# Output weight chunks moved into freed weight columns, 128-wide first scores, two weight waits, value products one place further behind

## The reference

```python
h = rmsnorm(x, norm_g)
proj = einsum('bsd,dp->bsp', h, w_in)          # q, k, v, gate of three groups, 8 heads of 64 each
o_sb = stick_breaking_attention(q, k, v)       # weights from sigmoids and a reverse cumulative product
o_ch = chunked_relpos_attention(norm(q), norm(k), v, rel_bias)   # softmax over own chunk + 8 before
o_fx = forgetting_attention(norm(q), norm(k), v, log_f)          # softmax with a decay, causal
mixed = concatenate([o_sb*silu(g_sb), o_ch*silu(g_ch), o_fx*silu(g_fx)])     # 1536 columns
return x + einsum('bsm,md->bsd', mixed, w_out)
```

## Time and profile before

| what | value |
|---|---|
| time, median of 3 runs | 1063.33 us (1063.33 to 1063.95) |
| time of the profiled execution | 1061.9 us |
| its span in the profile | 1060.1 us |
| granted TensorE clock, mean | 0.998 of full |
| PE busy | 1019.6 us, 96% |
| DVE busy / ACT busy | 680.4 us, 64% / 632.8 us, 60% |
| DMA traffic | 105.50 MB, 100 GB/s on average |

### The profile page before, as it was taken

One profiled execution on the slowest core, in us unless ns is written; L12 is line 12 of the kernel. 1 busy time (PEld: TensorE's weight loads), 2 busy tenths in 40 slices (PEclk: granted clock), 3 DMA queues, 4 the chain that ended last, 5 costly groups with the idle time before them and its releaser, 6 DMA issues.

```text
span 1060.1 us, 16214 instructions
## 1 busy us (share of the span) xinstructions
PE 1019.6 (96%) x5816; PEld 911.5 (86%) x5816; DVE 680.4 (64%) x1272; ACT 632.8 (60%) x1232; POOL 95.9 (9%) x74
## 2 busy tenths in 40 slices
PE   6999999999999999999999999999999997799998
PEld 5989989899899998998998998988988985677887
DVE  4656675765856656657557549789789677667210
ACT  5658775766767767758667667567566555444000
POOL 1210201101111011011011000011011010000000
PEclk9999999999999999999999999999999999999999
DMA  8244152331432413315314204214124137732941
GB/s 247 81 118 135 29 143 54 100 100 46 127 85 63 131 47 100 100 51 134 88 28 125 75 20 125 56 35 126 40 51 132 25 90 197 228 92 80 301 136 40
DMA packets 112944, 105.50 MB, mean 100 GB/s; under 512 B 10048, under 2 KB 83784, under 8 KB 112864
## 3 DMA queue, kind: packets, MB, share of 16 engines
q1 hardware_dynamic: 110432, 104.42, 35.5%
q10 hardware_dynamic: 2432, 0.05, 0.1%
HBM read 62.44 MB, written 19.98 MB: 78 GB/s over the span
## 4 chain that ended last, share of the span: by engine, by line
PE 77%; DVE 11%; ACT 5%; DMA 4%; issue 3%; SPq 1%; ACTq 0%; DVEq 0%
PE psP L1202 37%; PE psO L1294 8%; PE psT L1276 7%; PE psS L1254 4%; PE psP L1206 4%; PE psS L1255 4%; PE psP L1312 3%; PE psP L1342 2%; PE psS L1342 2%; DVE big L987 2%; PE psT L1224 2%; DMA stack<-stack 2%; PE psO L1342 2%; DVE pt L1117 1%; DVE rb L1106 1%
## 5 line engine op out<-in xcount | busy, mean ns | idle before, releaser
L1202 PE MATMUL psP<-big 128*128 128x384 f32 (+1 forms) x2304 | 478.8, 346 | 0.7 <-issue 0.5
L1202 PEld LDWEIGHTS psP<-big 128*128 128x128 f32 x2304 | 395.8, 189 | 7.2 <-issue 0.9
L1117 DVE TENSOR_TENSOR pt<-psT,pt 128x512 fp32r<-128x512 f32 (+1 forms) x224 | 143.3, 642 | 144.7 <-ACT pt L929 144.0
L929 ACT ACTIVATE pt<-psT 128x512 fp32r<-128x512 f32 (+1 forms) x224 | 124.9, 558 | 124.1 <-PE psT L1276 123.1
L1206 PE MATMUL psP<-big 128*128 128x512 f32 x576 | 157.2, 405 | 0.0
L1294 PE MATMUL psO<-pt,vst 128*128 128x512 f32 (+3 forms) x576 | 140.1, 343 | 8.4 <-DVE pt L1117 7.6
L1276 PE MATMUL psT<-identr,z 128*128 128x128 f32 x816 | 125.4, 272 | 0.0
L1206 PEld LDWEIGHTS psP<-big 128*128 128x128 f32 x576 | 102.0, 189 | 17.6
L1294 PEld LDWEIGHTS psO<-pt,vst 128*128 128x128 f32 x576 | 99.2, 189 | 20.6 <-issue 10.5
L1090 DVE CUSTOM_DVE_ANT_0 z<-psS,rb 128x640 f32<-128x640 f32 (+7 forms) x128 | 89.3, 698 | 39.5 <-PE psS L1255 20.4
L1276 PEld LDWEIGHTS psT<-identr,z 128*128 128x128 f32 x816 | 101.5, 140 | 15.3
(11 more groups left out here) (113 smaller groups left out, 1090.9 us busy)
## 6 DMA issues: line engine op xcount, KB each, us to landing
stack<-stack SPq DMA_DIRECT2D x192, 128.0 KB, 2.3
wraw<-in_w_in_dram SPq DMA_DIRECT2D x90, 192.0 KB, 2.6
wraw<-in_w_in_dram SPq DMA_DIRECT2D x24, 256.0 KB, 3.6
mixed_scratch<-mst SPq DMA_DIRECT2D x24, 256.0 KB, 2.7
mixed_scratch<-gate SPq DMA_DIRECT2D x24, 256.0 KB, 2.8
wraw<-in_w_out_dram SPq DMA_DIRECT2D x24, 256.0 KB, 2.8
rb<-decay_scratch SPq DMA_DIRECT2D x8, 512.0 KB, 4.1
big<-mixed_scratch SPq DMA_DIRECT2D x8, 512.0 KB, 6.1
```

The source lines that it names most:

```text
L929: nc.scalar.activation(pt[:, ci % PTR, 0, 0:w], psT[:, m % NT, 0:w], ACT.Copy).then_inc(s_hi, 1)
L1117: nc.vector.tensor_tensor(pt[:, ci % PTR, 1, 0:w], psT[:, m % NT, 0:w], pt[:, ci % PTR, 0, 0:w].bitcast(F32), ALU.subtract).then_inc(s_eva ...
L1202: ins = nc.tensor.matmul(dst[:, 0:TOKW - first], hT[a][:, k, i * P:(i + 1) * P], wpair[b][:, k, first:TOKW], start=(k == 0 and q == 0), st ...
```

## The change

Five things change.

1. `score_parts`: the first scores of a head are computed 128 wide instead of 256. The planner's cost of these steps falls with it.
2. `turned_steps`: the products of bank b stand behind the transposes of bank b+2, where it was b+1.
3. The weight waits at a pair's first token tile (except in the first pair): instead of one before each of 8 steps, one before step 0 for chunk 3 and one before step 4 for chunk 7.
4. The output weights: chunks 0 to 5 now go to the q, k, v columns of the input weights, which are free when the last token tile is projected (`s_tk`), and only from chunk 6 on does ACT wait for the gate (`s_gk`). These places and the next four (gate columns) are not one run of 512 columns but two of 256 or four of 128; the matmul reads its moving operand in these pieces (`shaped`). The planned places `WOUT` change: chunks 0 to 5 stand at 0.6 to 3.6, and 6 to 15 from 4.2 on 0.35 apart, where all 16 stood from 4.2 on 0.3 apart.
5. The output products: they may start at 4.2 instead of 5.5, and the two tiles of a pair of tiles no longer alternate step by step; the second starts 2.5 steps behind the first. `MIXF` changes slightly.

```diff
-        return at, [(at, k0 * P, max(w, 256))]
+        return at, [(at, k0 * P, w)]
...
+STAGGER = 2.5
+
+SOON = 6
...
-WOUT = [round(4.2 + 0.3 * c, 2) for c in range(EARLY)]
-FIRST_AT = 5.5
-MIXF = [2.8, 2.8, 7.0, 7.4]
+WOUT = [round(0.6 + 0.6 * c, 2) for c in range(SOON)] + [round(4.2 + 0.35 * c, 2) for c in range(EARLY - SOON)]
+FIRST_AT = 4.2
+MIXF = [2.7, 2.9, 7.0, 7.4]
...
-        seq += [("turn", u, b), ("values", u, b - 1)]
-    return seq + [("values", u, len(banks(u)) - 1)]
+        seq.append(("turn", u, b))
+        if b > 1:
+            seq.append(("values", u, b - 2))
+    return seq + [("values", u, b) for b in range(len(banks(u)) - 2, len(banks(u)))]
...
-    for i, k in [(i + b, k) for i in range(0, len(FIRST), 2) for k in range(MF) for b in range(2)]:
+    order = [(MF * (i // 2) + k + STAGGER * (i % 2) + 0.7 * (i // 2), i, k) for i in range(len(FIRST)) for k in range(MF)]
+    for _, i, k in sorted(order):
...
+        qkv_place = [wpair[i][:, k:k + 2, FW:FW + 256] for i in range(2) for k in range(0, KT, 2)]
+        qkv_place += [wpair[i][:, k:k + 4, FW + 256:TOKW] for i in range(2) for k in range(0, KT, 4)]
+        late_place = [wpair[i][:, k:k + 4, TOKW:WP] for i in range(2) for k in range(0, KT, 4)] + [
+            hT[i][:, k, HALF:SEQ] for i in range(2) for k in range(KT)]
+        places = qkv_place + late_place
...
+                wo[b][k][half] = places[2 * c + b] if c < EARLY else hT[b][:, c - EARLY, 0:HALF]
+
+        def shaped(flat, place):
+
+            return flat if len(place.shape) == 2 else flat.rearrange("p (a b) -> p a b", a=place.shape[1])
...
                     if step[1] == 0:
+                        act.wait_ge(s_tk, KT * PAIRS)
+                    if step[1] == SOON:
                         act.wait_ge(s_gk, KT * PAIRS)
...
-                        if gi == 0:
-                            pe.wait_ge(s_wlo, CHUNK["weights", j, k] + 1)
+                        if gi == 0 and (j == 0 or k % 4 == 0):
+                            pe.wait_ge(s_wlo, CHUNK["weights", j, k if j == 0 else k + 3] + 1)
...
-                            ins = nc.tensor.matmul(psP[:, i % 2, :], mixF[t][a][:, k, :], wo[b][k][c],
+                            ins = nc.tensor.matmul(shaped(psP[:, i % 2, :], wo[b][k][c]), mixF[t][a][:, k, :], wo[b][k][c],
```

More of the change, by code:

```diff
@@ L391, in build @@
         wpair = [big[:, w0 + i * KT * WP:w0 + (i + 1) * KT * WP].rearrange("p (k c) -> p k c", k=KT) for i in range(2)]
-        wo = [[[None] * 2 for _ in range(PAIRS)] for _ in range(2)]
[L395 to L403, removed]
+        qkv_place = [wpair[i][:, k:k + 2, FW:FW + 256] for i in range(2) for k in range(0, KT, 2)]
[3 more added lines that the diff above has]
+        places = qkv_place + late_place
+        wo = [[[None] * 2 for _ in range(PAIRS)] for _ in range(2)]
+        for c in range(24):
+            k, half = wout_at(c)
+            for b in range(2):
+                wo[b][k][half] = places[2 * c + b] if c < EARLY else hT[b][:, c - EARLY, 0:HALF]
+        def shaped(flat, place):
+            return flat if len(place.shape) == 2 else flat.rearrange("p (a b) -> p a b", a=place.shape[1])
         mixF = [[hT[h][:, :, t * P:(t + 1) * P] for h in range(2)] for t in range(FIRST_T)]
@@ L813, in _ @@
                     act.wait_ge(s_wld[CSLOT[c]], 16 * CUSE[c])
-                    nc.scalar.activation(wo[0][pos][half], wplace[CSLOT[c]],
+                    nc.scalar.activation(wo[0][pos][half], shaped(wplace[CSLOT[c]], wo[0][pos][half]),
                                          ACT.Copy).then_inc(s_whi, 1)
@@ L1009, in _ @@
                     dve.wait_ge(s_whi, c + 1)
-                    nc.vector.tensor_tensor(wo[1][pos][half], wplace[CSLOT[c]], wo[0][pos][half].bitcast(F32),
+                    nc.vector.tensor_tensor(wo[1][pos][half], shaped(wplace[CSLOT[c]], wo[1][pos][half]),
+                                            wo[0][pos][half].bitcast(F32),
                                             ALU.subtract).then_inc(s_wlo, 1)
@@ L1341, in _ @@
                         for q, (a, b) in enumerate(((0, 0), (0, 1), (1, 0))):
-                            ins = nc.tensor.matmul(endbank[g % 5], src[:, a, :], wo[b][k][c],
+                            ins = nc.tensor.matmul(shaped(endbank[g % 5], wo[b][k][c]), src[:, a, :], wo[b][k][c],
                                                    start=(k == k00 and q == 0), stop=(k == PAIRS - 1 and q == 2))
```

## The result

The changed kernel takes 1075.11 us (median of 6, 1072.16 to 1079.03) where the kernel before takes 1063.57 on the same chip: ratio 1.0109, 95% interval 1.0088 to 1.0129. It is slower by 11.5 us (1.1%); I had forecast 1048. The profiled execution took 1072.18 us.

What follows compares the result with a forecast made beforehand. PE, busy 96% of the span, and the moments in which it stands were taken as the bound. 1061.9 - 1.7 - 6 - 0 - 7.1 = 1047.1 us; with 1.4 for the median 1048.5, stated as 1048, range 1040 to 1059.

Steps and rivals of the forecast that it cites:

- The value products: Products one bank further behind: half of 11.5 us of PE waits close, 6 us gained; ends 11.5 gain, 3.5 loss.
- rival two: Attention part: blocked ACT starts copies late, DVE idles then lags; the 6 us stay out, 1054.5 us; chance 0.13.
- The output stretch: Early chunks and earlier output products: 16 us lost before, less 8.9 us of other limits, 7.1 us won.
- Chunk waits: Output products: PE's waits for chunk subtractions fall from 10.8 us to under 4.
- the mixed values: Output start: PE waits for their loads, 2.0 us for the first tile, up to 1.0 for the second; sum 3.
- so 2 us: Output, fifth tile: PE waits 2 us for the residual's addition, rows landing 4 to 5 us after issue.
- The clock: Output: granted clock stays 1.00 between 880 and 925 us; the 1.6 us lost at 0.50 before count as won.
- First scores: 24 first scores 128 wide: 0.07 us less a head, 1.7 us gained on PE; ends nothing and 2.8.
- Weight waits: Two waits in place of eight at a pair's first tile: zero, with an end of +1.4 us.
- Rival four (pieces): Output products of chunks 4 to 7: PE reads four pieces like four matmuls; 1057 or 1070 us; chance 0.06.

Runs made afterwards that it cites:

- e1: The changed kernel with the value products back at one bank behind, all other edits kept: 1060.27 us, ratio 0.9966 to the kernel before.
- e2: The kernel before with only the value products two banks behind (units 0 to 43; last four units as before): 1082.34 us, ratio 1.0168.
- e5: The changed kernel with value products one bank behind in units 3, 7, 11 and so on, two behind in the other 36: 1063.41 us, ratio 0.9990.
- e9: The changed kernel with value products two banks behind only in units 3, 7, 11 and so on, one behind elsewhere: 1071.00 us, ratio 1.0093.
- e10: e1 with the next pair's head transposes placed later, behind one more score and one more bank: 1076.28 us, ratio 1.0120 to the kernel before.
- e12: The changed kernel once more, unaltered, for a second profile: profiled execution 1076.94 us.
- e4: The kernel before with the output edits alone (chunk places and times, earlier start, second tile 2.5 steps behind): 1060.63 us, ratio 0.9970.
- e8: e1 with the second residual load issued ahead of mixed values 2 and 3: 1055.52 us, ratio 0.9917 to the kernel before.
- e6: The kernel before with the first scores 128 wide in place of 256, alone: 1063.84 us, ratio 1.0003.
- e7: The kernel before with first scores 128 wide and two weight waits in place of eight: 1063.30 us, ratio 0.9996.

## Why the prediction was wrong, point by point

**The value products: -6 forecast, +15 to +18 measured (e1, e2).** The step that failed reads: "But that dependence stood before as well, and then those transposes came after these products; the copy starts no later than before relative to the products it waits for." Relative to its products it starts no later; relative to everything else on PE it does, because the products themselves moved back behind whatever stood between the banks. In one unit of four that is the head transposes and a score. The sentence ahead of it named what queues behind the blocked copy, "sigmoids, raw copies", and left out the one with the least slack, the head copy: two pairs of transfers and the next pair's scores hang on it. What I had priced at nothing measured 10.3 us of stack waits and 3.9 us of head transposes waiting for a bank. e5 and e9 place all but 2.6 us of the loss in those units, e10 shows that the delay of this chain is enough by itself. By the Trainium skill ("TensorE: Matmul & The Clock Gate", section "Architectural detail", on engine queue depths) ScalarE and VectorE are strictly first in, first out. The trace agrees, with the head copy 2.6 us behind its transposes' start. The gain side was right in kind (7.6 to 1.9 us), and rival two had the blocked ACT, but followed it to DVE and not to the head copy, and priced it as eating 6 us, no more.

**The rest of that loss, the clock.** I had counted the slow clock only where it stood before. Behind small regular waits stand new stretches at 1.2 GHz, outside the output work: five in e2's profile, two in each of e9's, e10's and e12's, none in the changed kernel's first. No step of the sum had a term for it.

**The output stretch: -7.1 forecast, -3.2 measured (e4).** Chunk waits went to nothing and the mixed values cost 2.3 to 3.3 for my 3: right. Mis-sized was "so 2 us" for the residual rows: 5.3 us in e4. I let the rows land 4 to 5 us after issue, and 13 us after SP began the second loads of mixed values. In e4 SP begins those at 900.8, needs 3.5 us to issue the three rows, and DVE adds at 916.96: 9.2 us after the first row's issue and 16 after that of the mixed values. The 3 us between 13 and 16 are about what my wait was short by (3.3):

```profile
907.74 3.51 SPq L674 DMA_DIRECT2D raw<-in_x_dram  x3
...
916.96 0.69 DVE L1161 TENSOR_TENSOR raw<-psP,raw 128x512 f32<-128x512 f32 x1 [4.79 <-DMA raw<-in_x_dram]
```

The clock, which I had forecast at 1.00, missed by as much: I had counted the slow 3.4 us of before as won (1.6 us), and e4's profile has 10.2 us at 0.50 about the two waits, with PE at work in 7.6 of them, which is 3.8 us lost.

```profile
881.20:884.60 3.40, 3.26 (x9) 2.05 (x8) 0.66 (x1) 0.10 (x1) 0.00 (x0) 0.50 1.10 331
915.30:922.10 6.80, 4.30 (x12) 3.55 (x13) 2.40 (x4) 0.60 (x1) 0.00 (x0) 0.50 0.57 143
```

e8 moves the mixed values from ahead of the residual rows to behind them and gets 5.2 us.

**First scores: -1.7 forecast, 0 measured (e6).** The matmuls are as cheap as I said: starts 0.06 and 0.11 us apart in place of 0.115 twice, about 60 ns a head and 1.4 us over 24. Two exposed weight loads, as I had worked them out from the Trainium skill ("TensorE: Matmul & The Clock Gate", section on LDWEIGHTS), would have made 0.21; it is 0.17. What the step left out is that PE then meets its next wait sooner: work taken off an engine need not be time. That this is where the 1.4 us went is argued, not shown.

```profile
303.24 0.22 PE L1269 MATMUL psS<-stack 128*128 128x128 f32 x1
303.30 0.28 PE L1270 MATMUL psS<-stack 128*128 128x128 f32 x1
303.41 2.31 PE L1217 MATMUL psP<-big 128*128 128x384 f32 x12
```

**Weight waits: 0, with an end of +1.4. Right (e7).** **Rival four (pieces) is false:** successive output products that read four pieces start 233 ns apart at full clock (median of 40), those that read one piece 231 (77), and 231 before. The slower case came by another way than the one I gave 0.06.

**The sum.** By the parts, -6 became +15 (e1), -7.1 became -3.2 (e4) and -1.7 became 0 (e6), some 27 us in all. That is the distance from 1048 to 1075, so no large term is missing.

## What to carry to other kernels

Before you move a step in an order written for several in-order engines, list for each instruction that now waits longer everything queued behind it, and follow the one with the least slack (here a small copy that starts a chain of two pairs of transfers) to its consumer; an engine that is idle for 40% of the time can still sit on the path. A wait removed counts only as far as the next one, and where a load is late, look at what stands ahead of it in the queue: moving the three loads of residual rows past the last four loads of mixed values gave more than the whole rework of the output stretch. Keep what helps (e8: 1055.5 us) and drop the shift.

## What the runs showed of the hardware

The granted clock fell behind single waits of TensorE, and not each time: in e2 five waits of 1.7 to 2.0 us, and in e9 one of 1.52, were followed by 3.4 us at 0.50, while in the changed kernel's first profile waits of 1.77 us at 145.5 and 1.79 at 736.5 were not. The changed kernel's six executions spread over 6.9 us, against 2.6 us for the kernel before on the same chip; in the three groups of experiments, with 11 to 29 executions, the kernel before spread over 4.1 to 5.8. Two 128-column score matmuls after one another start 58 ns apart (57 to 60 in 22 of 24 places, 134 and 136 in two), with 109 to 120 ns to whatever follows. And a 512-column matmul whose moving operand lies in four runs of 128 starts its successor as soon as one with a single run, 233 against 231 ns.
